# One core of a hybrid decoder step: semaphores of the first loads, the closing passes of the sample's top keys, and the first tile's experts chosen in three parts

## What is computed

```python
# h = RMSNorm(x); x1 = x + W_out [A(h); B(h)]; y = x1 + PEER(RMSNorm(x1))
# one input projection h @ w_in gives all of A's and B's inputs
# A: an indexer scores the keys, each query attends to its best k = min(256, L/4) of them
_, idx = lax.top_k(where(causal, index_scores(qi, wi, ki), -inf), k_top)     # 128 (prompt), 256 (sample)
# B: latent attention over all keys, from compressed rows
# PEER, for each token, 8 heads:
s = einsum('thpd,hpnd->thpn', q, peer_sub_keys)         # 2 x 128 scores per head
sv, si = lax.top_k(s, 16)
cand = sv[:, :, 0, :, None] + sv[:, :, 1, None, :]       # 256 sums
cv, ci = lax.top_k(cand, 16)                             # 16 experts per head, e = their numbers
g = softmax(cv)
act = gelu(einsum('td,thkd->thk', xb, peer_u[e]))        # one 4 KB row per token and expert
y = einsum('thk,thkd->td', g * act, peer_v[e])           # and another
```

## Time and profile before

| what | us |
|---|---|
| median of 3 runs | 2349.43 (2338.41 to 2356.35) |
| the profiled execution | 2348.06 |
| its span, first to last instruction | 2346.3 |
| TensorE busy in the span | 1763.5 |
| VectorE busy | 1610.7 |
| GpSimd busy | 1234.0 |
| ScalarE busy | 989.6 |
| clock granted to TensorE, mean share of 2.4 GHz | 0.807 |
| moved by DMA | 695.64 MB, mean 296 GB/s |

### The profile page before, as it was taken

How to read it: one execution, slowest core, us unless ns; L and a number is a source line. 1 busy time by engine, 2 the same in 40 slices (tenths; PEclk the granted TensorE clock), 3 DMA queues, 4 the chain that set the end, 5 groups by cost and what they waited for, 6 DMA issues and landing times.

```text
span 2346.3 us, 26214 instructions
## 1 busy us (share of the span) xinstructions
PE 1763.5 (75%) x8918; PEld 1299.5 (55%) x8918; DVE 1610.7 (69%) x3641; ACT 989.6 (42%) x1711; POOL 1234.0 (53%) x1251
## 2 busy tenths in 40 slices
PE   7995999638858967987877977847876976753556
PEld 3553657327646756665655755636654655543445
DVE  2546682887876777778676786786887778677441
ACT  1223343133544323555665664643342443233345
POOL 1000000367666666666667666656566656767664
PEclk9997799858977857978978987977987887875667
DMA  7001202499998989999999999979899889999997
GB/s 256 24 11 38 56 1 73 156 354 405 351 342 331 346 312 353 354 359 370 344 361 392 372 354 385 344 262 389 314 354 376 314 325 348 373 401 348 358 372 283
DMA packets 191573, 695.64 MB, mean 296 GB/s; under 512 B 26192, under 2 KB 28624, under 8 KB 188368
## 3 DMA queue, kind: packets, MB, share of 16 engines
q0 software_dynamic: 178608, 674.33, 76.2%
q1 hardware_dynamic: 12832, 19.65, 2.8%
HBM read 690.14 MB, written 3.76 MB: 296 GB/s over the span
## 4 chain that ended last, share of the span: by engine, by line
PE 42%; DVE 21%; issue 12%; POOL 6%; ACT 6%; another core or an unknown queue 5%; DVEq 4%; DMA 4%; ACTq 0%; POOLq 0%
PE ps L2230 8%; PE ps L2037 7%; DVE region L1690 6%; POOL region L682 6%; DVEq L1097 4%; DVE xall L1701 3%; DMA region<-in_peer_v,region 3%; PE ps L1722 2%; ACT region L1086 2%; PE ps L2054 2%; PE ps L1987 2%; PE ps L2130 1%; PE ps L2019 1%; PE ps L2082 1%
## 5 line engine op out<-in xcount | busy, mean ns | idle before, releaser
L682 POOL DMA_INDIRECT region<-in_peer_u,region x507 | 515.7, 1017 | 611.6 <-DVEq L1097 440.1
L2230 PE MATMUL ps<-ident,region 128*128 128x128 f32 x3312 | 552.7, 325 | 262.4 <-issue 138.1
L682 POOL DMA_INDIRECT region<-in_peer_v,region x571 | 571.7, 1001 | 335.2 <-issue 145.8
L1690 DVE SCALAR_TENSOR_TENSOR region<-region,h_now 128x1024 f32<-128x1024 f32 x507 | 611.7, 1214 | 116.5 <-DMA region<-in_peer_u,region 69.6
L2230 PEld LDWEIGHTS ps<-ident,region 128*128 128x128 f32 x3312 | 472.1, 169 | 350.6 <-issue 204.3
L1086 ACT ACTIVATE region<-region 128x1024 f32<-128x1024 f32 x414 | 464.9, 1139 | 245.0 <-DMA region<-in_peer_v,region 189.0
L2037 PE MATMUL ps<-w_uk_s,region 128*128 128x512 f32 x544 | 294.3, 669 | 8.7 <-issue 6.7
L1701 DVE SCALAR_TENSOR_TENSOR xall<-region,xall 128x1024 f32<-128x1024 f32 x157 | 201.7, 1285 | 20.9 <-issue 4.7
L2037 PEld LDWEIGHTS ps<-w_uk_s,region 128*128 128x128 f32 x544 | 106.3, 218 | 91.8 <-issue 88.2
L946 ACT ACTIVATE region<-ps 128x512 f32<-128x512 f32 x136 | 80.2, 590 | 163.5 <-PE ps L2037 101.3
L953 ACT ACTIVATE region<-ps 128x256 f32<-128x256 f32 x136 | 51.5, 379 | 202.2 <-remote 115.0
(11 more groups left out here) (404 smaller groups left out, 2824.5 us busy)
## 6 DMA issues: line engine op xcount, KB each, us to landing
region<-in_w_peer_q POOLq DMA_DIRECT2D x31, 512.0 KB
region<-in_peer_v,region POOLq DMA_INDIRECT x571
region<-in_peer_u,region POOLq DMA_INDIRECT x507
region<-in_w_in POOLq DMA_DIRECT2D x8, 882.0 KB, 14.8
region<-in_w_peer_q SPq DMA_DIRECT2D x8, 512.0 KB, 4.7
region<-in_x_turned SPq DMA_DIRECT2D x5, 512.0 KB, 3.5
region<-in_w_out SPq DMA_DIRECT2D x2, 1024.0 KB, 12.4
region<-in_w_out SPq DMA_DIRECT2D x1, 2048.0 KB, 18.3
```

The source lines that it names most:

```text
L682: pool.indirect_dma_start(ring[r][:], None, table, bass.IndirectOffsetOnAxis(ap=experts[:, t, n:n + 1], axis=0)).then_inc(landed[r], 16)
L1690: v.scalar_tensor_tensor(ring[r][:], ring[r][:], 1.0, h_now[:], ALU.mult, ALU.mult, accum_out=acts[:, t % 2, n:n + 1]).then_inc(S["u_done" ...
L2230: last = te.matmul(ps[6 + c // 4][:, (c % 4) * P:(c % 4 + 1) * P], ring[r][:, c * P:(c + 1) * P], ident[:], is_transpose=True, start=(m == ...
```

## The change

Four edits.

1. **First loads.** w_in's eight blocks are counted on four semaphores as 1, 2, 3 and 2 blocks instead of 2 each. g_cq gets a semaphore of its own, so VectorE's scaling waits for the norm's gains alone; ident is loaded ahead of the first rows of x.
2. **First tile in three parts.** Heads 0 and 1 before the loop (14 marks in each of the last two units, 6 behind them), heads 2 and 3 as `c0q` in steps 0 to 13, heads 4 to 7 as `c0b` in steps 16 to 41. `chosen` counts one more from then on, and GpSimd waits for it at entries 0, 32 and 64 of tile 0. Since the lists of two heads don't lie side by side, their places are picked by `lists`. r1 moves from steps 38 to 53 into 42 to 55, c1 from 54 to 97 into 56 to 97.
3. **Closing passes.** Counting is done by the product itself (scalar_tensor_tensor with accum_out, the second operand one column broadcast), the mask is kept as what is left out, in units of NONE = -2^100, and the last product writes it. Nine passes over the scores become six.
4. **Order behind them.** `sel` gets steps 351 to 361 instead of 351 to 355; a_init, y1, a0 to a7, lat, mixS, r4 and c4 follow five to six steps later (a0 starts in step 366 for 361, c4 in 498 for 493). The SHARES and chain_b keep their steps.

```diff
--- before.py
+++ after.py
@@ -37,6 +37,7 @@
 EPS = 1e-6
 NEG = -1e30
 TAKEN = -3e38
+NONE = -2.0 ** 100
 G = HA // KVA
 KTOP_P = min(256, SEQ // 4)
 KTOP_S = min(256, (PAST + NT) // 4)
@@ -262,7 +263,10 @@
 
         ident_in = sem("ident_in")
         g_mix_in = sem("g_mix_in")
+        g_cq_in = sem("g_cq_in")
         const_in = sem("const_in")
+
+        W_IN = [0, 1, 1, 2, 2, 2, 3, 3]
         w_in_in = [sem(f"w_in_in{i}") for i in range(4)]
         x0_in = sem("x0_in")
         x_in = sem("x_in")
@@ -361,16 +365,17 @@
 
         MB = 2 * (NPG + 4) + 15
         MA, MI, MR, MC, MX = 24, 8, 19, 34, 10
+        MK = 10
         C_PAGES = [(0, 6), (6, 12), (12, NPG + 1)]
         chain_b = [(f"b{b}", 36 + 55 * b, 36 + 55 * b + 50, MB) for b in range(NB)]
 
         MIXED_AT = LAG
         NBIT = 31
         chain_t = [("top", 166, 351, 2 * (NBIT + 1) + 4)]
-        chain_a = [("c0b", 0, 36, MC), ("r1", 38, 54, MR), ("c1", 54, 98, MC), ("idx", 100, 160, NB * MI), ("rows", 160, 164, 6),
+        chain_a = [("c0q", 0, 14, MC), ("c0b", 16, 42, MC), ("r1", 42, 56, MR), ("c1", 56, 98, MC), ("idx", 100, 160, NB * MI), ("rows", 160, 164, 6),
                    ("y0", 164, 167, 3), ("r2", 167, 184, MR), ("c2", 184, 244, MC), ("r3", 258, 275, MR), ("c3", 275, 351, MC),
-                   ("sel", 351, 356, 10), ("a_init", 356, 357, 2), ("y1", 357, 359, 3)]
-        at = 361
+                   ("sel", 351, 362, MK), ("a_init", 362, 363, 2), ("y1", 363, 365, 3)]
+        at = 366
         for b in range(NB):
             if b == NB - 2:
                 chain_a.append(("y2", at, at + 2, 3))
@@ -462,9 +467,9 @@
 
             load_xT(0)
             sp.dma_start(g_cols[:, 0:KD], a["g_norm_mix"]).then_inc(g_mix_in, 16)
-            sp.dma_start(g_cols[:, KD:], a["g_cq"]).then_inc(g_mix_in, 16)
+            sp.dma_start(ident[:], a["c_ident"]).then_inc(ident_in, 16)
             sp.dma_start(xall[:, 0, :], a["x_prompt"][0, 0:P, :]).then_inc(x0_in, 16)
-            sp.dma_start(ident[:], a["c_ident"]).then_inc(ident_in, 16)
+            sp.dma_start(g_cols[:, KD:], a["g_cq"]).then_inc(g_cq_in, 16)
             sp.dma_start(rope_a[:], a["c_rope_a"]).then_inc(const_in, 16)
             sp.dma_start(rope_b[:], a["c_rope_b"]).then_inc(const_in, 16)
             sp.dma_start(causal[:], a["c_causal"]).then_inc(const_in, 16)
@@ -487,7 +492,7 @@
             sp.dma_start(g_heads[:, 1, :], row("g_k_a", DH)).then_inc(const_in, 16)
 
 
-            sp.wait_ge(w_in_in[2], 32)
+            sp.wait_ge(w_in_in[2], 16 * W_IN.count(2))
             sp.wait_ge(xT_ready, 1)
             load_xT(1)
             sp.wait_ge(w_in_in[3], 32)
@@ -606,7 +611,7 @@
         def _(pool):
 
             for c in range(KD):
-                pool.dma_start(w_in[:, c, :], a["w_in"][c * P:(c + 1) * P, :]).then_inc(w_in_in[c // 2], 16)
+                pool.dma_start(w_in[:, c, :], a["w_in"][c * P:(c + 1) * P, :]).then_inc(w_in_in[W_IN[c]], 16)
             pool.dma_start(w_uq[:], a["w_uq"].rearrange("(c p) n -> p c n", p=P)).then_inc(weights_in, 16)
             pool.dma_start(w_uk[:], a["w_uk"].rearrange("(c p) n -> p c n", p=P)).then_inc(weights_in, 16)
             pool.dma_start(w_uv[:], a["w_uv"].rearrange("(c p) n -> p c n", p=P)).then_inc(weights_in, 16)
@@ -667,9 +672,9 @@
                 elif f >= W_OUT_AT:
                     pool.wait_ge(S["o_up"], 4 + f - W_OUT_AT + 1)
                 if kind == "u" and n == 0:
-                    pool.wait_ge(S["chosen"], t + 1 + (t > 0))
-                if kind == "u" and t == 0 and n == P // 2:
-                    pool.wait_ge(S["chosen"], 2)
+                    pool.wait_ge(S["chosen"], t + 3 if t else 1)
+                if kind == "u" and t == 0 and n in (P // 4, P // 2):
+                    pool.wait_ge(S["chosen"], 2 if n == P // 4 else 3)
                 if kind == "w":
                     pool.dma_start(ring[r][:], a["w_peer_q"][n * P:(n + 1) * P, :]).then_inc(landed[r], 16)
                 elif kind == "o" and n < G:
@@ -773,7 +778,7 @@
             act.wait_ge(x0_in, 16)
             x_square(0)
             x_scale(0)
-            act.wait_ge(g_mix_in, 32)
+            act.wait_ge(g_cq_in, 16)
             keep_projected(0)
             for t in range(NTILE - 1):
                 project(t)
@@ -905,7 +910,7 @@
 
                 def keep_s(j, bank):
                     act.wait_ge(S["routed"], 4 * t + j + 1)
-                    hold(act, S["chosen"], t + 1)
+                    hold(act, S["chosen"], t + 2)
                     rows, x = slice(0, P), 4 * j
                     if packed:
                         rows, x = slice(NTOK * (j // 2), NTOK * (j // 2) + NTOK), 4 * (j % 2)
@@ -934,7 +939,7 @@
                 yield
                 yield
 
-            all_of(gate(1, 0, PH // 2))
+            all_of(gate(1, 0, PH // 4))
 
             def mixer_b(b):
                 n0 = (NPG + 1) * b
@@ -1059,8 +1064,8 @@
             parts = {f"b{b}": mixer_b(b) for b in range(NB)}
             parts.update({f"a{b}": mixer_a(b) for b in range(NB)})
             parts.update({f"r{t}": route(t, packed=t == 4) for t in range(1, NTILE)})
-            parts.update({f"c{t}": gate(t + 2, 0, PH if t < 4 else PH // 2) for t in range(1, NTILE)})
-            parts.update(c0b=gate(2, PH // 2, PH), idx=index(), rows=index_rows(), top=top_keys(), sel=chosen_keys(), lat=latent())
+            parts.update({f"c{t}": gate(t + 3, 0, PH if t < 4 else PH // 2) for t in range(1, NTILE)})
+            parts.update(c0q=gate(2, PH // 4, PH // 2), c0b=gate(3, PH // 2, PH), idx=index(), rows=index_rows(), top=top_keys(), sel=chosen_keys(), lat=latent())
 
             def take_sums(t):
                 act.wait_ge(S["v_added"], pe_rows(pe_ends(t)[1]) + 1)
@@ -1184,7 +1189,7 @@
                 settle()
                 v.tensor_tensor(qb[:], qb[:], g_qk[:, 0:1, :].broadcast_to([P, HB, DQK]), ALU.mult).then_inc(up_normed, 1)
 
-            dve.wait_ge(g_mix_in, 32)
+            dve.wait_ge(g_mix_in, 16)
             scale_x(0)
             x_norm(0)
             scale_x(1)
@@ -1258,8 +1263,9 @@
 
             def choose_experts(t, h0=0, h1=PH):
                 heads = h1 - h0
-                count = t + (1 if t or h0 else 0) + 1
-                dve.wait_ge(S["s_kept"], 4 * t + 4 if t or h0 else 2)
+
+                count = t + 3 if t else 1 + 4 * h0 // PH
+                dve.wait_ge(S["s_kept"], 4 * t + 4 if t or h1 > PH // 2 else 2)
                 if t == 0 and h0 == 0:
                     dve.wait_ge(S["o_turned"], 3)
 
@@ -1297,7 +1303,9 @@
                     yield
 
                 where = [(4 * (x // 8) + x % 4, x // 4 % 2) for x in range(2 * PH)]
-                yield from top16(lambda x: sv[:, where[x + 2 * h0][0], where[x + 2 * h0][1], :], lambda x: si[:, where[x + 2 * h0][0], where[x + 2 * h0][1], :], lambda x: s_pk[:, x + 2 * h0, :], 2 * heads)
+                lists = [x for x in range(2 * PH) if h0 <= where[x][0] < h1]
+                yield from top16(lambda x: sv[:, where[lists[x]][0], where[lists[x]][1], :], lambda x: si[:, where[lists[x]][0], where[lists[x]][1], :],
+                                 lambda x: s_pk[:, lists[x], :], 2 * heads)
                 for i0, i1, w, at in ((0, 4, TK, 0), (4, TK, 4, 4 * TK)):
                     n = i1 - i0
                     v.tensor_tensor(cand[:, h0:h1, at:at + n * w].rearrange("p h (i j) -> p h i j", i=n), sv[:, h0:h1, 0, i0:i1].unsqueeze(3).broadcast_to([P, heads, n, w]),
@@ -1357,7 +1365,7 @@
                 settle()
                 yield
 
-            choosing = choose_experts(0, 0, PH // 2)
+            choosing = choose_experts(0, 0, PH // 4)
             for n in range(NU):
                 blk, kind, nk, q, keys, values, chunk, col, scale = unit(n)
                 mask = sel[:, blk - 1, 0:nk] if kind == "a" and blk else seen[blk]
@@ -1395,13 +1403,13 @@
                 if n in NORM_0:
                     next(norming)
                 if n >= NU - 2:
-                    for _ in range(8):
+                    for _ in range(14):
                         next(choosing)
             out(NU - 2)
             invert(NU - 1)
             settle()
             out(NU - 1)
-            for _ in range(MC - 16):
+            for _ in range(MC - 28):
                 next(choosing)
 
             def mix_rest():
@@ -1557,14 +1565,17 @@
                 yield
 
             def chosen_keys():
-
-                greater, equal, order = (w[0:NTOK, :] for w in masks)
+                n = PAST + NT
+
+                left_out, equal, order = (w[0:NTOK, :] for w in masks)
                 first, second = t_two[0:NTOK, 0:1], t_two[0:NTOK, 1:2]
-                v.tensor_scalar(greater, scores, first, None, ALU.is_ge)
-                settle()
-                yield
-                v.tensor_reduce(trial_sum[0:NTOK], greater, AX, ALU.add)
-                settle()
+                one, none = t_pos[0:NTOK], t_sign[0:NTOK]
+                v.memset(one, 1.0)
```

(33 more changed lines are left out.)

## The result

The changed kernel takes 2372.57 us, median of 4 runs (2362.87 to 2385.23), against 2346.41 for the kernel before in the same session: ratio 1.0095, 95% interval 1.0048 to 1.0142. A second comparison, in another session, gave 1.0037 (1.0006 to 1.0068). So the change costs 0.4 to 1%, where 0.5% gained was forecast; 2372.57 lies above the range's end of 2360. The profiled execution took 2385.23 us with a span of 2383.4, the longest of the four. (A ratio leaves out executions over 1.5% above the fastest of their kernel, so it can differ from the quotient of the medians.)

The account below looks back on a forecast made before the run. No engine was taken as the bound everywhere; the end hung on when VectorE finishes the last choice. Gains 0.4 + 5.4 + 3.3 + 2.5 = 11.6 us off 2348.1 gave 2336.5, with 1.4 for the median 2338; range 2324 to 2360.

Parts of the forecast that it names:

- the advance: First tile: choosing two heads before the loop brings the first gather 11.4 us earlier, to 430.2, and dot 0 to 436.
- 20.2 for 17.4, so dot 22 is 6 us early: Steps 16 to 21: VectorE's marks, dots and adds take 20.2 us instead of 17.4, leaving dot 22 6 us early.
- 34.2 us: Steps 22 to 37: they run at the gathers' pace, 34.2 us as before, so dot 38 is still 6 us early.
- rival (b): First 100 steps: VectorE is often the bound and the lead is paid back; 2342 to 2347, say 2345; chance 0.2.
- between nothing and 2 x 3.3 us … I take 4.5: Tile 1's choice, two steps later: two more steps of TensorE's work ahead of it cost 4.5 us.
- 5.4 us forecast: First tile's net gain at dot 98: 6 - 4.5 + 3.9 = 5.4 us; bounds 11.4 gained and 4.1 lost.
- The term that was short: Closing passes: the strided pass takes 2.36 us, within 15.1 us for six passes against 19.9 before, 4.8 less.
- That isn't a loss of its own: those five steps were made earlier: Last choice, five steps later: GpSimd waits some 18 us instead of 6.36 without loss, the steps being made in the spread-out passes.
- 3.3 us off for the first scores: After the closing passes: shorter waits for turned sums and first scores, 20 us instead of 24.2, gain 3.3; bounds nothing and 7.
- 2.5 for the shares: VectorE's share of the v rows: 2.4 fewer lie beside the attention and last choice, 2.5 us gained.
- Rival (c): Steps 357 to 362 held by something other than VectorE's passes, such as pages; attention five steps later, 16 us: 2357; chance 0.15.
- Start: First loads: the second projection begins at 37.2 instead of 37.65, a gain of 0.4 us, at most 0.5.

Follow-up runs that it names:

- start_alone: Kernel before with only the first loads' semaphores and order changed (edit 1): ratio 0.9989 to the kernel before.
- three_alone: Kernel before with only the first tile in three parts and tile 1's routing and choice moved (edit 2): ratio 0.9973.
- moved_alone: Kernel before with only tile 1's routing moved to steps 42 to 55 and its choice from 56, first tile in two halves: ratio 1.0002.
- pages_early: Changed kernel with the first batch's keys and values fetched three steps earlier in GpSimd's order: ratio 1.0033 to the kernel before.
- c4_long: Kernel before with only the last choice spread five steps longer, over steps 493 to 511: ratio 1.0029.
- c4_short: Changed kernel with the last choice in steps 498 to 503 instead of 498 to 511: ratio 1.0055 to the kernel before.
- early_attention: Kernel before with edits 1 and 3, closing passes and attention five steps earlier, last choice in its old steps, faster chip: 2127.48 us, ratio 0.9949.
- early_form_again: Kernel before with edits 1 and 3 and the order five steps earlier, on the faster chip: 2128.55 us against 2139.67, ratio 0.9954.
- c0b_from_22: Kernel before with edit 2, but heads 4 to 7 chosen in steps 22 to 41 instead of 16 to 41: ratio 1.0052.

## Why the prediction was wrong, point by point

**First tile: the advance is right, its survival is not.** The first gather came at 431.54 (430.2 forecast), dot 0 at 437.2 (436), dot 16 at 473.1 (472). The step that failed is the next: "20.2 for 17.4, so dot 22 is 6 us early". It measured 25.2, and 24.8 to 26.5 in all seven profiles with it. The window of these six steps in the kernel before and after, over all engines:

```profile
480.80:498.10 17.30, 0.37 (x2) 0.37 (x3) 12.07 (x35) 7.49 (x7) 5.90 (x7) 0.50 0.78 300
```

```profile
473.10:498.30 25.20, 0.37 (x2) 0.37 (x3) 17.84 (x67) 8.18 (x8) 11.07 (x12) 0.50 0.79 316
```

VectorE is busy 17.8 us, which is no more than the 20.2 of work that I had added up (with overlapping lengths counted twice it is 21.4). The other 7.4 are idle time, nearly all with no known releaser, and it was 7.1 to 8.9 us in all seven. I had put it at nothing, though the same steps had 5.2 us of it in the kernel before. Over dots 0 to 22 the seven stand idle for 9.9 to 11.1 us, and the kernels with the old first tile for 5.8 to 8.5 (1.0 on the faster chip of the last section). The next 16 steps repeat this: I forecast 34.2 us, VectorE was busy 34.4 and they took 40.2, so dot 38 came at 538.5 (526 forecast). From dot 22 to 42 it evens out (52.4 for 53.3). From dot 0 to dot 22 every kernel with three parts and c0b from 16 lost the 11 us by which it led: of the 12.4 between start_alone and three_alone 7.4 are work (the 4.1 that I had counted for the third part and, as the remainder, 3.3 of the later heads' passes drawn ahead of dot 22) and 5.0 more standing still. I had named as rival (b) that VectorE keeps the books, and given it 0.2; it has the outcome, and some three fifths of the mechanism.

The second term, "between nothing and 2 x 3.3 us … I take 4.5" for the moved routing, was mis-sized: 42 to 64 takes 79.4 to 91.6 us with it and 71.4 to 79.6 without, 11 on the means, and moved_alone shows it with the old first tile. I priced two steps of TensorE's work and left out that ScalarE and VectorE are queued behind the same routing, and that the choice's first mark now comes while the routing's last scores aren't kept (14.29 and 4.56 us). It shows no cost in the end, since 64 to 346 got 8 us shorter (mean 898 for 906), barely more than single profiles spread. That isn't VectorE's work either: it was busy 668 to 671 us of that stretch in every kernel, and the difference is idle time. At dot 351 the six profiles with c0b from 16 and the normal place of the search stand at 1545.6 us on the mean, the eight with the old first tile at 1545.5 (1535 to 1562 singly). So of the 5.4 us forecast nothing is seen there, within some 4; the ratio of three_alone by itself (0.9973, 9 us to either side) couldn't tell.

**Closing passes: form right, one term short.** The products with sum took 2.35 and 2.34 us, as forecast. The Trainium skill's rule of the half rate (Vector Engine (DVE) Microarchitecture Reference, Points that are easy to get wrong) would have made 4.7 of them; the trace doesn't agree, and the dot product itself would have shown it beforehand: it has two float32 inputs in SBUF and a sum, at 1.22 us for 1,024 columns. The term that was short is the last: the strided pass with two inputs took 3.63 us, not the 2.36 of the strided one with one input, so the passes are 16.4 us and save 3.5 of 4.8. The buffers were cleared 38.9 us after dot 351 (41 forecast).

**The five later steps: the step that decides.** The forecast says of the last choice's wait "That isn't a loss of its own: those five steps were made earlier", took 3.3 us off for the first scores and 2.5 for the shares (2.4 rows of 1.28 us are 3.1). The wait was as forecast (19.9 for 18), the time behind it too (232.5 for 230). But edit 4 alone costs 10 us (0.03 to 0.79%), and the changed kernel without it equals the kernel before, within 9 us. The order the other way, five steps earlier, gained 0.5 to 0.7% in three comparisons (always with edits 1 and 3) and 0.0 to 0.1% in two (0.4 and 0.6% by the medians). The first scores came after 69.5 to 76.7 us with the new passes and the later order, after 62.5 to 70.6 with the old order: 60 to 62 was never there.

The profiles show where most of the loss arises. Up to the first scores the five with new passes and the later order need 72.6 us on the mean, the two with new passes and the old order 64.7; with the old passes it is 81.0 in one for 68.5 on the mean of seven. So the later order costs 8 to 12 us up to here, where the forecast had 3.3 gained. From the first scores to the last tile's gather nothing comes back (518 us on the mean of the four with the same last choice, 517 on that of seven with the old order), although in these 143 dots VectorE does weight fewer rows, 75 for 78, and is busy 389.7 us for 395.4: what I had for the shares was work saved, and no time.

I had argued that what counts is when those steps run; the steps do run early (dots 351 to 368 in 59.4 us for 78.9), but the next sixteen take 75.2 us for 56.1, so by dot 384 nothing is left in this pair (134.6 us for 135.0), with the attention five steps behind. A gain in dots is no gain while the attention hasn't begun.

Rival (c) had the right sign, named the attention later by five steps, and gave it 0.15; its place was wrong (steps 351 to 362 took 36.3 us, not over 53), and its means, the pages, aren't borne out by pages_early. That its 2357 lies near what 0.4% more than the kernel before would be is luck, as its means don't hold.

**What stays open.** The profiles put edit 4's loss ahead of the first scores, but on single executions, and why TensorE and ScalarE reach them so much later isn't shown. What the work moved ahead of the choice (five dots and three rows, 10 us of VectorE's time at 0.3 to 0.8) and GpSimd's longer wait add isn't separated in time. c4_long leaves all open, c4_short speaks against the wait, early_attention speaks against the last choice's place, and that only on the faster chip. Nor was the cause of the first comparison's larger loss found: it and the second overlap only from 1.0048 to 1.0068.

**Start.** 37.17 for 37.2, the second projection's first matmul; ratio of the edit 0.9989. On the way there the forecast was off and it cost nothing: scaling began at 4.42, not 9.05, so TensorE's first matmul came at 7.04, not 10.3, and then waited 0.42 and 1.72 us for pieces of w_in. (25.3 us by eight are 3.2, not 3.0.)

## What to carry to other kernels

An order written out in steps has two prices: when the work is done, and how many steps stand ahead of the part that comes last; try it in both directions before touching the instructions, since here five steps later cost some 10 us and five earlier gained up to 17, while three edits of code came to nothing that could be measured. Date a forecast by when the last part begins, not by step numbers. A lead early in a long loop has to survive the next stretch: add up the busiest engine's work there and the idle time that the trace of before already shows in those steps, which doesn't vanish because more work is put in. Where chance moves a single execution by 0.4%, a stall of one profile is a place to look, not a price.

## What the hardware showed that was not expected

**One chip was 9% faster for the three kernels that ran on it, and had next to no unexplained stalls.** The kernel before took 2346 to 2372 us in five sessions and 2140 in the sixth. Windows over dots 98 to 160 and ScalarE's waits by releaser show where. Dots 98 to 160 in the kernel before, first session:

```profile
726.40:952.00 225.60, 183.99 (x921) 141.07 (x921) 163.29 (x231) 79.38 (x170) 143.16 (x138) 0.73 0.90 329
```

The same dots of early_form_again, on the faster chip:

```profile
697.70:883.40 185.70, 165.14 (x898) 125.74 (x898) 163.08 (x230) 75.01 (x163) 140.36 (x133) 0.81 1.00 389
```

VectorE's work is the same to 0.2 us; the gathers run at 389 GB/s for 329, TensorE is granted 0.81 for 0.73 of its clock, and 62 steps take 40 us less. What ScalarE waited for from 450 us on, the kernel before:

```profile
ACT region L1086 <- DMA region<-in_peer_v,region: 189.0, 82, 13.0
ACT region L953 <- remote: 115.0, 33, 8.5
```

and early_form_again (us in total, times, longest):

```profile
ACT region L1089 <- DMA region<-in_peer_v,region: 412.6, 235, 9.6
```

On the faster chip, with its DMA engines busy 1.00 of the time in dots 98 to 160, ScalarE's waits are mostly for gathers; in the kernel before much of that turns into waits on nothing known. Counting idle times over 0.3 us with "issue" or "remote" behind them from 450 us on, VectorE has 209.8 us of them in the kernel before and 2.6 in early_form_again, ScalarE 426.7 and 1.7. The stall of 17 to 20 us in pages_early and the instructions of c0b_from_22 that come 1.4 us apart where they usually come 0.2 apart are such pieces. What makes them isn't shown, nor what else ran on those chips: the Trainium skill (Runtime: NRT & Kernel Launch, Instruction fetch mechanics) says that the cost of loading instructions is mostly hidden, and no run here shows such loading by itself. They aren't all chance either, as the 7.1 to 8.9 us in the same six steps of seven profiles show. A forecast from one profile prices them as if they were fixed to the place where they fell, which is what I did with the 6.84 us of idling ahead of MAX8: at that place, ahead of MAX8 in step 54, the eight other profiles on these chips had 3.7 to 14.3 us, and the two on the faster chip none.
